# GpSimd also makes the low halves of the branch and merge panels in both attention layers

## What is computed

```python
def hybrid_layer(x, ...):
    ...
    a = causal_depthwise_conv(a, conv_a_w) + conv_a_b          # 31 taps
    a = jax.nn.silu(layer_norm(a, ln_a_g, ln_a_b))
    y_a = (a * jax.nn.silu(a_gate)) @ w_a_out                  # branch0
    y_b = (yb * jax.nn.silu(b_gate)) @ w_b_out                 # branch1
    y_c = (o * jax.nn.silu(c_gate)) @ w_c_out                  # branch2
    g_a, g_b, g_c = jnp.split(jax.nn.sigmoid(merge_logits), 3, axis=-1)   # merge0, merge1, merge2
    m = g_a * y_a + g_b * y_b + g_c * y_c
    return layer_norm(DEEPNORM_ALPHA * x + gate * (m @ w_o), ln_g, ln_b)
```

## Time and profile before

| | |
|---|---|
| median of 3 runs | 1282.26 us (1279.92 to 1282.38) |
| profiled execution, its own time | 1279.57 us |
| its span in the trace | 1277.8 us |
| PE / PEld busy | 86% / 79% of the span |
| DVE / ACT / POOL busy | 65% / 44% / 12% |
| low halves on DVE (line 1003) | 115, 254.4 us busy |
| low halves on POOL (line 696) | 32, 149.7 us busy |

### The profile page before, as it was taken

One profiled execution on the slowest core, in us unless ns is written; L12 is line 12 of the kernel. 1 busy time (PEld: TensorE's weight loads), 2 busy tenths in 40 slices (PEclk: granted clock), 3 DMA queues, 4 the chain that ended last, 5 costly groups with the idle time before them and its releaser, 6 DMA issues.

```text
span 1277.8 us, 20030 instructions
## 1 busy us (share of the span) xinstructions
PE 1099.2 (86%) x8056; PEld 1013.0 (79%) x8056; DVE 836.3 (65%) x1736; ACT 561.3 (44%) x638; POOL 156.6 (12%) x59
## 2 busy tenths in 40 slices
PE   5688988668979999987978898999899787989995
PEld 4685756548869999977967788998689586989985
DVE  4818999975545432235697879566456977795662
ACT  5225555533344443435523264454355233635532
POOL 2000000000039688730000000000000000000000
PEclk7896777778889999998988899999999798999998
DMA  8333232326727555546514243655356042535610
GB/s 256 96 111 115 84 129 70 100 81 212 234 71 259 166 198 180 184 133 197 178 54 133 99 135 123 194 177 165 115 183 200 31 139 93 165 127 170 198 35 33
DMA packets 159436, 179.57 MB, mean 141 GB/s; under 512 B 4976, under 2 KB 141680, under 8 KB 159344
## 3 DMA queue, kind: packets, MB, share of 16 engines
q1 hardware_dynamic: 159024, 177.22, 43.4%
q0 software_dynamic: 320, 1.07, 0.3%
HBM read 177.23 MB, written 1.05 MB: 140 GB/s over the span
## 4 chain that ended last, share of the span: by engine, by line
PE 45%; DVE 34%; issue 9%; ACT 8%; DMA 2%; POOL 1%; SPq 0%; DVEq 0%; ACTq 0%; POOLq 0%
PE pg L1494 14%; PE pg L1496 13%; PE pg L1495 13%; DVE area L1394 7%; DVE area L1012 4%; DVE area L1175 4%; ACT w_hi L732 3%; DVE w_lo L1003 3%; DVE area L1181 3%; DVE area L1184 3%; DVE area L1020 2%; ACT area L711 2%; DMA raw<-in_w_in 2%; POOL w_lo L696 1%; PE p_s L1584 1%
## 5 line engine op out<-in xcount | busy, mean ns | idle before, releaser
L1494 PE MATMUL pg<-u_hi,w_hi 128*128 128x256 f32 x1664 | 498.8, 300 | 53.4 <-DVE u_lo L1012 36.9
L1495 PE MATMUL pg<-u_lo,w_hi 128*128 128x256 f32 x1664 | 488.3, 293 | 0.0
L1496 PE MATMUL pg<-u_hi,w_lo 128*128 128x256 f32 x1664 | 487.1, 293 | 0.0
L1494 PEld LDWEIGHTS pg<-u_hi,w_hi 128*128 128x128 f32 x1664 | 337.5, 203 | 65.3 <-issue 43.7
L1003 DVE TENSOR_TENSOR w_lo<-raw,w_hi 128x2048 fp32r<-128x2048 f32 (+3 forms) x115 | 254.4, 2218 | 128.1 <-ACT w_hi L732 127.9
L1495 PEld LDWEIGHTS pg<-u_lo,w_hi 128*128 128x128 f32 x1664 | 337.5, 203 | 0.8
L1496 PEld LDWEIGHTS pg<-u_hi,w_lo 128*128 128x128 f32 x1664 | 336.8, 202 | 0.0
L732 ACT ACTIVATE w_hi<-raw 128x2048 fp32r<-128x2048 f32 (+2 forms) x147 | 272.7, 1858 | 97.7 <-PE pg L1496 36.6
L696 POOL TENSOR_TENSOR w_lo<-raw,w_hi 128x2048 fp32r<-128x2048 f32 x32 | 149.7, 4698 | 395.5 <-ACT w_hi L732 395.5
L738 ACT ACTIVATE area<-pg 128x512 f32<-128x512 f32 (+2 forms) x92 | 54.0, 587 | 172.5 <-PE pg L1496 159.2
L1394 DVE SCALAR_TENSOR_TENSOR area<-area,par 128x256 f32<-128x256 f32 x240 | 97.8, 481 | 0.8
(11 more groups left out here) (185 smaller groups left out, 1402.0 us busy)
## 6 DMA issues: line engine op xcount, KB each, us to landing
raw<-in_w_in SPq DMA_DIRECT2D x68, 1024.0 KB, 5.4
raw<-in_w_ff SPq DMA_DIRECT2D x32, 1024.0 KB, 5.7
raw<-in_w_ada SPq DMA_DIRECT2D x24, 1024.0 KB, 5.2
raw<-in_w_gate SPq DMA_DIRECT2D x8, 1024.0 KB, 6.7
raw<-in_w_o SPq DMA_DIRECT2D x8, 1024.0 KB, 5.3
raw<-in_w_out SPq DMA_DIRECT2D x4, 1024.0 KB, 7.5
raw<-in_w_b_out SPq DMA_DIRECT2D x4, 1024.0 KB, 5.0
raw<-in_w_c_out SPq DMA_DIRECT2D x4, 1024.0 KB, 5.2
```

Source lines behind the costliest of these rows:

```text
L1494: pe.matmul(dst, w_h, x_h, start=first, stop=False)
L1495: pe.matmul(dst, w_h, x_l, start=False, stop=False)
L1496: return pe.matmul(dst, w_l, x_h, start=False, stop=last_)
```

## The change

Six job names are added to the tuple. The panels so named are 18 in each of the two layers: two of each branch, four of each merge. Their low halves leave DVE's list and join POOL's. Nothing else differs.

```diff
-POOL_LOW = ("ff1", "ff2")
+POOL_LOW = ("ff1", "ff2", "branch0", "branch1", "branch2", "merge0", "merge1", "merge2")
```

## The result

The changed kernel took 1346.21 us (median of four runs, 1343.2 to 1350.04), the kernel before 1282.32 us beside it (four runs, 1279.92 to 1286.89). The ratio is 1.0495, with a 95% interval from 1.0451 to 1.0540: 64 us slower, by about 5%. The median is inside the predicted range of 1308 to 1348, but by 2 us only, and 1 us above the 1328 to 1345 that rival A gave itself; two of the four runs lie above 1348. Rival A had the right places but one. The missing place cost 13.5 us, of which terms that were too large took back some 5, so that the number came near is partly luck.

What follows compares the result with a forecast made beforehand. PE, busy for 86% of the span, was taken to bound the kernel. Stalls and slower clock of 28.0 us per layer, 56 for two, on 1279.6 gave 1335.6, or 1338 by the median; forecast 1336 us, range 1308 to 1348.

Steps and rivals of the forecast that it cites:

- rival A: Whole kernel: stalls at the convolution and at `branch0`, each with a slower clock behind; 1336 us, 1328 to 1345, chance 0.62.
- The mechanism: DVE instructions with two SBUF inputs and POOL operations reading SBUF exclude one another, the later blocking for the whole other.
- D: Exclusion does not bind for these tiles; the convolution ends earlier, 3.6 us saved per layer, 1275 us, chance 0.04.
- E: No change: the five POOL operations fall outside the convolution or cost what they save; chance 0.02.
- C: At the convolution, running taps keep POOL out until all are done; +13.8 us per layer, 1310 us, chance 0.08.
- B: Only the convolution's stall, as `vb_lo` slips through at `branch0`; 41 us in all, 1323 us, chance 0.20.
- Term 1: First layer's convolution: five POOL operations of 4.65 us delay the taps, so `merge1` panel 2 starts 18.2 us later.
- Term 2: PE behind the convolution's stall: half clock costs 2.5 us per layer, between 1.5 and 3.5.
- Term 3: At `branch0`, `vb_lo` waits in turns with POOL: PE stalls 5.3 us, then loses 2.0 to the clock, per layer.
- The sum: Per layer 18.2 + 2.5 + 5.3 + 2.0 = 28.0 us, two layers 56, added to the execution before.

Runs made afterwards that it cites:

- the subtractions: Against the kernel before, DVE keeps all its low halves and POOL adds two unused 128 x 1024 subtractions per moved panel: 1348.45 us against 1283.47.
- memsets: Against the kernel before, DVE keeps all its low halves and POOL adds five write-only 128 x 1024 memsets per moved panel: 1289.69 us, ratio 1.0058.

## Why the prediction came out as it did

**The mechanism** was right for instructions with two inputs in SBUF: DVE and POOL take turns, one whole instruction each. An operation that reads PSUM stays out of it: beside the subtractions, DVE's `area<-pg,area` at 770.24 took its 0.69 us during POOL's two from 766.38 to 772.35. Rivals D and E fell with the row of 38 taps, C with POOL's getting in among them (at 780.88, 796.75 and 802.50), and B with the stall at `branch0`, which came in both layers.

**Term 1, the convolution**, was a little too large, 18.2 us for 16.2: PE's stall grew by 16.7 us, from 3.09 to 19.76, and the 0.5 us between the sums and the next panel, which DVE's low half had cost, is gone. All five POOL operations fell into it, as worked out. From the first tap to the last it took 25.1 us before and 41.8 now. Each operation cost DVE 4.3 us (4.24 for `va_lo`, 17.26 for four in the 38 taps), where I had taken 4.65. POOL's own five durations add up to 24.4 us, more than the 21.5 that DVE lost.

**Term 2, the clock**, was taken as 2.5 us and measured 1.8. The text has the clock at 0.50 behind the stall; it was at that level for the sums, and 0.81 in the mean to the panel's end. In all `merge1` panel 2 took PE 18.0 and 17.7 us longer in the two layers, and terms 1 and 2 had said 20.7.

**Term 3, the operand of `branch0`**, with its clock, said 7.3 us and was 7.2 and 7.9.

**The step that failed** is the cost of `branch1`. The text follows only its panel 1 ("near 763") and looks only at what that does to `vb_lo` and the taps. The low half of panel 0, which comes first, it never places, and that one meets the two divisions for the last heads. The sum puts one-input instructions at nothing. The prediction says that no run shows their exemption and that the sum does not use it, but to leave them out was to use it. The runs show the contrary: 4.95 us for two in place of 0.68, PE 4.15 us without work, a spell at half clock behind, together +7.0 and +6.5 us. The Trainium skill (SBUF — State Buffer, section Who interferes with whom) exempts a one-input VectorE instruction only outside the two-port modes, and names `tensor_scalar` among those that can enter them and then contend; I had quoted the exemption without its condition. With the condition the trace of the divisions agrees: memsets hold them up and not the taps. No row names a mode, but three rows bear on it (kernel before, DVE by form, 750 to 900 us; busy us, mean ns of one):

```profile
L1016 DVE TENSOR_SCALAR area<-area,par 128x256 f32<-128x256 f32 x4 | 1.7, 414 | 0.1
...
L1016 DVE TENSOR_SCALAR area<-area,rsum 128x256 f32<-128x256 f32 x2 | 0.7, 353 | 0.1
L1016 DVE TENSOR_SCALAR area<-area,rsum 128x128 f32<-128x128 f32 x2 | 0.6, 288 | 0.1
```

For 128 more values a division takes 65 ns more; a two-input product takes 135 (0.69 us for 512, 1.23 for 1024), so the divisions run about twice as fast. The four of the first row, in `ln_a_var`, take 414 ns, as long as a tap of the same size, and are held up all the same. Whether the rule covers them no run here shows.

**The sum.** Twice 28.0 us, plus 13.5 for the missing place, less 5.7 for terms 1 and 2, plus 0.5 for term 3, gives 64.3, and the medians differ by 64. The profiled execution has some 6 us more. About 3.5 of them lie ahead of anything that the change touches; 1.6 at `branch2` and 1.0 at `w_o` stand in the first layer alone, in stretches of lower clock, and are not explained further.

**Left open:** which of the one-input operations are held up. Those of line 1016 with input and output in SBUF that met POOL are (four of them in `ln_a_var` took 10.15 us in all, off PE's path). Two other kinds, at lines 1339 and 1392 of the changed kernel, keep means of 407 and 408 ns, but they run only in stretches in which POOL has nothing to do, so they say nothing either way.

## What to carry to other kernels

Before work goes from DVE to POOL, list what DVE does while POOL runs. For each POOL operation that will fall among DVE instructions of two SBUF inputs, or one-input multiplications like the divisions, and that PE will wait for, add nearly its whole duration (4.3 us of 4.6 here); what DVE saves counts only where its own copy stood on the path. If POOL has to be used, place its operations over DVE's idle time or its reads of PSUM (0.69 us beside POOL as without it): one wait of under a microsecond was worth 16.5 us here. Where DVE is late by a few microseconds at one point, first try to write the order so that PE asks one panel later, which cost nothing here and gave 8.2 us.

## What the runs showed of the hardware that was not expected

A POOL operation that only writes (memset, 128 x 1024, 1.0 us) also holds up one-input multiplications on SBUF: the four of `ln_a_var`, with a mean of 414 ns without POOL, have 973 ns beside it. Two-input operations lose nothing to it, at 479 ns for a tap and 2288 ns for a low half.

A stall of 3.1 us lowers PE's clock in one execution and not in another: the eight sums took 1.99 us in the kernel before and 3.78 us with `branch1` moved, and also with `merge2` and `branch0` moved, which come later, behind the same wait of 3.08 or 3.09 us. That is 1.8 us that the last of these edits cannot have put there. It may be one source of this kernel's scatter of a few microseconds; no run was made to show it.
